# Decay of the old sample state: from GpSimd to VectorE, in a one-step hybrid decoder layer

## The reference

```
u  = beta * (v - exp(g) * (k @ S))                # the correction, one row of 128
o  = exp(g) * (q @ S) + (q . k) * u               # the output of the token
S' = S * exp(g) + outer(k, u)                     # the new state, an output of the program
```

```
S = S * gl_i[..., None, None] + jnp.einsum('bhck,bhcv->bhkv', kd_i, u)
```

## Time and profile before

| | us |
|---|---|
| median of the runs | 1510.76 (3 runs, 1509.71 to 1514.75) |
| the profiled execution, its own time | 1514.65 |
| its span, from the first to the last instruction | 1512.7 |
| time of it outside the span | 1.95 |
| busy: TensorE / VectorE / ScalarE / GpSimd | 1326.8 / 495.3 / 430.3 / 149.2 |
| mean granted TensorE clock | 0.924 of full |

### The profile page before, as it was taken

The page is one execution under the profiler, slowest core; times in us unless marked ns, Lnnn a source line. Parts: engine busy times, 40 slices in busy tenths (PEclk is TensorE's granted clock), DMA queues, the critical chain, the costliest instruction groups (busy, mean ns, idle before and its releaser), DMA issues.

```text
span 1512.7 us, 23789 instructions
## 1 busy us (share of the span) xinstructions
PE 1326.8 (88%) x10377; PEld 1049.6 (69%) x10377; DVE 495.3 (33%) x813; ACT 430.3 (28%) x760; POOL 149.2 (10%) x202
## 2 busy tenths in 40 slices
PE   4999999999999999884499697599999999999954
PEld 3999899888989999884398596345445444544434
DVE  5333433322334665546523625410101010101014
ACT  4434222532433444442433524101101101011011
POOL 2400000000011221204010121000100010001000
PEclk9999999999999999975577898799999999999975
DMA  5223344175113221240320232399999999999943
GB/s 207 95 90 115 109 168 196 57 306 196 56 57 92 84 72 69 63 128 0 139 77 8 100 143 69 154 387 431 428 431 431 432 430 431 429 431 429 405 96 84
DMA packets 58604, 307.31 MB, mean 203 GB/s; under 512 B 29314, under 2 KB 33794, under 8 KB 36515
## 3 DMA queue, kind: packets, MB, share of 16 engines
q1 hardware_dynamic: 56227, 301.98, 50.7%
q0 software_dynamic: 2304, 4.26, 0.7%
HBM read 289.51 MB, written 20.84 MB: 205 GB/s over the span
## 4 chain that ended last, share of the span: by engine, by line
PE 69%; DMA 16%; DVE 7%; ACT 6%; issue 1%; POOL 0%; DVEq 0%; ACTq 0%; POOLq 0%
PE pp L743 35%; DMA e_up<-in_w_up 15%; PE pp L964 13%; PE pp L954 3%; PE pp L812 2%; PE pp L1164 2%; PE pp L726 2%; ACT u_diag L1471 1%; PE pp L1252 1%; PE pp L1099 1%; PE pp L1117 1%; PE pp L1127 1%; PE pp L853 1%; PE pp L833 1%; PE pp L1191 1%
## 5 line engine op out<-in xcount | busy, mean ns | idle before, releaser
L743 PE MATMUL pp<-ht_h,w_h 128*128 128x260 f32 x1280 | 264.5, 288 | 10.9 <-DVE ht_l L1844 9.1
L743 PE MATMUL pp<-ht_h,w_l 128*128 128x260 f32 x1280 | 258.7, 284 | 0.0
L743 PE MATMUL pp<-ht_l,w_h 128*128 128x260 f32 x1280 | 258.3, 283 | 0.0
L743 PEld LDWEIGHTS pp<-ht_h,w_h 128*128 128x128 f32 x1280 | 198.9, 190 | 16.5 <-issue 14.2
L743 PEld LDWEIGHTS pp<-ht_h,w_l 128*128 128x128 f32 x1280 | 198.2, 189 | 0.0
L743 PEld LDWEIGHTS pp<-ht_l,w_h 128*128 128x128 f32 x1280 | 198.0, 189 | 0.0
L1737 DVE TENSOR_TENSOR w_l<-raw,w_h 128x2048 fp32r<-128x2048 f32 x52 | 120.4, 2317 | 119.0 <-ACT w_h L1272 119.0
L964 PE MATMUL pp<-e_down,act_t 128*64 128x512 f32 x512 | 113.4, 595 | 18.5 <-ACT act_t L1581 18.5
L954 PE MATMUL pp<-sel,h2p 104*128 104x128 bf16 x2040 | 118.6, 221 | 10.7 <-DVE sel L2223 10.7
L954 PEld LDWEIGHTS pp<-sel,h2p 104*128 104x128 bf16 x2040 | 116.0, 99 | 10.8 <-DVE sel L2223 10.8
L1272 ACT ACTIVATE w_h<-raw 128x2048 fp32r<-128x2048 f32 x52 | 99.2, 1909 | 82.3 <-PE pp L743 34.4
(11 more groups left out here) (418 smaller groups left out, 1730.6 us busy)
## 6 DMA issues: line engine op xcount, KB each, us to landing
e_gate<-in_w_gate SPq DMA_DIRECT2D x16, 4096.0 KB, 19.8
e_down<-in_w_down SPq DMA_DIRECT2D x32, 2048.0 KB, 13.3
e_up<-in_w_up SPq DMA_DIRECT2D x16, 4096.0 KB, 22.6
raw<-in_w_blk SPq DMA_DIRECT2D x52, 1024.0 KB, 4.9
kv_ring<-in_cache_k SPq DMA_DIRECT2D x8, 1024.0 KB, 7.3
kv_ring<-in_cache_v SPq DMA_DIRECT2D x8, 1024.0 KB, 6.6
yt<-y_rows SPq DMA_DIRECT2D x5, 832.0 KB
s<-in_state_gdn SPq DMA_DIRECT2D x1, 4096.0 KB, 13.3
```

Of the source, the lines that this page charges most:

```text
L743: last = mm(dst, w_[s][:, k, cs], x_[:, k, ts], start=(k == 0 and q == 0), stop=(k == KD - 1 and q == 2))
```

## The change

GpSimd no longer does the 8 multiplications by the decay. VectorE does each of them directly ahead of the addition of the same head, so that `sd_add` now is multiply, wait for the multiply, add. The semaphore `sd_dec` goes. The wait that stood ahead of GpSimd's first multiplication (until `sd_state` is through) stands ahead of VectorE's first one. `link` makes VectorE wait for its own last instruction. Nothing else is changed; the numbers are the same.

```
-        sd_rhs, sd_u, sd_o, sd_diag, sd_dec, sd_new = (sem(n) for n in ("sd_rhs", "sd_u", "sd_o", "sd_diag",
-                                                                       "sd_dec", "sd_new"))
+        sd_rhs, sd_u, sd_o, sd_diag, sd_new = (sem(n) for n in ("sd_rhs", "sd_u", "sd_o", "sd_diag",
+                                                                       "sd_new"))
...
-                elif e == "sd_outer":
-                    h = ev[1]
-                    if h == 0:
-                        pool.wait_ge(side_free, SIDE[("sd_state",)] + 1)
-                    tt(s0[:, h, :, :], s0[:, h, :, :], s_bc[:, 1, :, h:h + 1].to_broadcast([128, NS, 128]),
-                       ALU.mult).then_inc(sd_dec, 1)
...
                 elif e == "sd_add":
                     h = ev[1]
+                    if h == 0:
+                        dve.wait_ge(side_free, SIDE[("sd_state",)] + 1)
+                    link(tt(s0[:, h, :, :], s0[:, h, :, :], s_bc[:, 1, :, h:h + 1].to_broadcast([128, NS, 128]),
+                            ALU.mult))
                     dve.wait_ge(sd_outer_mm, h + 1)
-                    dve.wait_ge(sd_dec, h + 1)
                     tt(s0[:, h, :, :].rearrange("p (a b) n -> p a (b n)", a=2), pp[h % 4][:],
                        s0[:, h, :, :].rearrange("p (a b) n -> p a (b n)", a=2), ALU.add).then_inc(sd_new, 1)
```

## The result

The changed kernel takes 1493.9 us in the median of 4 runs (1490.98 to 1495.54), the kernel before 1510.24 (4 runs, 1508.91 to 1514.75). The ratio is 0.9884 with a 95% interval of 0.9857 to 0.9911: faster by 13 to 22 us. The forecast was 1498.2 with a range of 1494.5 to 1503.5. The interval of the gain, 13 to 22 us, begins just above 12.5.

What follows compares the result with a forecast made beforehand. VectorE, held to GpSimd's pace from 694.01 to 710.03 us, was taken as the bound. Removing that gives 12.91 us, about 0.4 goes to added multiplications: 1510.76 - 12.53 = 1498.2 us, range 1494.5 to 1503.5.

Steps and rivals of the forecast that it cites:

- The chain and its cause: From 694.01 to 714 us the chain of waits lies on VectorE, slowed by GpSimd's multiplications, which read SBUF.
- The eight slow instructions: L2018, L2019 and six of the inversion on VectorE, 694.01 to 710.03 us, about 2 us each whatever their size.
- the six inversion steps: VectorE's slow inversion instructions of 231 to 247 numbers, forecast to take 2.66 us together without the slow pace.
- The sum of the stretch: Up to the recurrence: 12.91 us less slow pace, about 0.4 us of added multiplications seen, 12.53 us gained.
- The estimate of 1.13 us: Time of one new VectorE multiplication by the skill page's 58 cycles and one per number; 1.225 was taken instead.
- ScalarE would not come last: Ahead of L1820, ScalarE's second copy of `u_st` ends at 699.73, 0.14 us before VectorE is ready.
- Behind 747.20 nothing changes but the start: From the recurrence's start on, everything including the expert weight loads just moves earlier, by 12.5 us.
- The prediction's own sign of being wrong: TensorE's recurrence taking over 3 us more or less than its 125.3 us would show the forecast wrong.
- The clock as a rival: TensorE's clock levels in the recurrence shift by a 5 us stretch, worth 2.5 to 5 us: 1494.5 or 1502; 8%.

Runs made afterwards that it cites:

- e3: The kernel before with the eight multiplications by the decay left out altogether; 1493.74 us, ratio 0.9901.
- e8: The changed kernel with GpSimd again doing its eight multiplications at the old place, into a scratch tile nobody reads, VectorE's staying; 1508.76 us.
- e9: The changed kernel with 16 GpSimd memsets of a scratch tile at the old place of its multiplications; 1492.92 us in one run.
- e4: The changed kernel with twelve 128x1024 copies put on VectorE ahead of L2012, a delay of 8.7 us; 1508.3 us, ratio 0.9991.
- e7: The kernel before with three VectorE maxima ahead of the last addition, a delay of 1.4 us; 1506.85 us, ratio 0.9984.
- e1: The kernel before, unchanged, run again with a second profile; 1508.9 us.
- e10: The changed kernel with a second buffer for `u_diag`, so that ScalarE and TensorE no longer take turns; 1493.26 us, ratio 0.9871.
- e2: The changed kernel, unchanged, run again with a second profile; 1493.29 us, ratio 0.9895.

## Why the prediction missed, step by step

- **The chain and its cause: right.** The eight slow instructions were held up by GpSimd's (e3, e8), and by its reading, not its writing (e9). What the prediction's sum calls "the six inversion steps" are six instructions, the multiplication and the subtraction of three steps (231, 240 and 247 numbers). The run of j = 10 to 15 has six steps, and the last three already ran at 0.4 us. The 2.66 us for the six instructions are right.
- **The sum of the stretch: right to 0.1 us.** 12.53 us were forecast, 12.56 measured; 12.91 without any multiplication, 12.93 in e3. A multiplication took 1.215 us (forecast 1.225), a pair 2.39. The estimate of 1.13 us from the table in the Trainium skill's page "VectorE: DVE Perf Modes", section "The TRN2 errata", is not borne out. The same section says that this row of its table comes out too low and gives (N + 151) / 0.96 ns for an fp32 operation of this kind, an estimate of 1.224 us, with which the measured 1.215 agrees; the estimate in the prediction was made with the other one. That ScalarE would not come last held too. This is the group of the new multiplications, in the stretch from 716 to 737 us:

```profile
L2029 DVE TENSOR_TENSOR s<-pp,s 128x1024 f32<-128x1024 f32 x8 | 9.8, 1224 | 0.3
L2026 DVE TENSOR_TENSOR s<-s,s_bc 128x1024 f32<-128x1024 f32 x8 | 9.7, 1215 | 0.0
```

- **"Behind 747.20 nothing changes but the start": this step failed.** It puts everything behind the stretch at no difference, and takes a shift of 12.5 us for harmless. The gain in the medians was 16.3 and 15.6 us, 3 to 4 more than the shift, and e4 (15.0 us for a shift of 8.7) and e7 (2.6 us less for a delay of 1.4) show that a shift is not passed on one for one. What differs in the profiles is the granted clock: in the twelve profiles of kernels whose recurrence has the same instructions (before, after, e1 to e10) the stage took 114.2 to 125.4 us. The two of the changed kernel have 114.4 and 116.4, the two of the kernel before 125.4 and 115.6. The prediction's own sign of being wrong, a recurrence over 3 us away from 125.3, was there. How the 3 to 4 us divide between the recurrence and what lies behind it is not measured; e1 had 3.0 us of its excess behind.
- **The clock as a rival: right in kind, too small a chance.** It had 8% and a price of 2.5 to 5 us "in either direction", down to 1494.5, and the medians came out at such a price, 3 to 4 us. Between two single executions it is more: 10.9 us between the first two profiles. Most of that is the one stretch of 17 us, in which the lower level got through 81 matmuls and the upper through 163, so that it cost about 8.5 us (an estimate from these two rows). It may also be unequal in its directions: a kernel whose profile shows such a stretch seems to have more to win by being moved than to lose. The rows for that were there: a recurrence with a mean clock of 0.75, and a profiled execution 3.9 us above its median.
- **The range** ended at 1494.5, 4 us below the forecast, for a kernel whose three known runs spread over 5 us. It should have gone as far down as the stretch at the lower level allowed.

What stays open: whether it is the place against the clock that gives the 3 to 4 us in the medians, and if so, why this place is nearly the same in so many executions. If it were random, a fixed shift should not matter in the median beyond its own length, and e4 and e7 show that it does. In 12 of the 14 profiles the short rise of the clock near 697 us comes 2.1 to 3.7 us behind the second row of the `u` computation (5.3 and 5.4 in e2 and e3), so the two seem to be tied; no run isolates how.

## What to carry to other kernels

When a run of short VectorE instructions takes the same time whatever their size, look at what GpSimd is reading: moving idle-looking work off GpSimd can shorten VectorE although it adds to it. Count such a gain from the waits that set the end, then ask where the added work meets the next bound (here 0.4 of 9.7 us were seen, and the cover was then gone). And where a later TensorE stage runs at two clock levels, do not take a shift for neutral: compare several profiles, and widen the range by what one whole stretch at the lower level costs.

## What the runs showed of the hardware

- A wait of 1.4 us just ahead of a TensorE stage made one kernel 2.6 us faster (0.9984, 0.9969 to 0.9998). In the other the median rose by 5.7 us, or 3.6 by the ratios, whose intervals overlap.
- The same 725 or so matmuls of the recurrence took 114.2 to 125.4 us in twelve profiles, at a mean granted clock of 0.81 to 0.75.
- GpSimd's multiplications (2.06 us each) held VectorE instructions with two SBUF operands to about 2.0 us each (1.8 to 2.1); 16 us of GpSimd memsets held none. The exclusion is not strictly one for one: in e8 one step took 0.39 us in the middle of the slow ones, probably in the gap between two GpSimd instructions, which wait for each other there.
- A 128x1024 copy from SBUF to SBUF took 0.72 us when it ran along the row (e4: 8.70 us for twelve) and 1.04 us when it transposed within the row, less than the 1.22 us of a two-operand operation of the same size.
